# Attention with the probabilities stationary and all query tiles first, and a recurrent layer whose gate tiles run among its convolution tiles

## The reference

```python
# first block, attention: q and k are normed and rotated first
sc = jnp.einsum("bqgrd,bkgd->bgrqk", qi, k).astype(jnp.float32) * scale
p = jax.nn.softmax(sc, axis=-1).astype(v.dtype)
return jnp.einsum("bgrqk,bkgd->bqgrd", p, v)

# second block, recurrent layer
h = rms_norm_2(x, norm_g)
u = h @ w_in
xb, gate = u[..., :D_RNN], u[..., D_RNN:]
xb = causal_depthwise_conv(xb, conv_w, conv_b)
r = jax.nn.sigmoid(... xblk, w_rg ... + b_rg)
i = jax.nn.sigmoid(... xblk, w_ig ... + b_ig)
log_a = -LRU_C * r.astype(jnp.float32) * jax.nn.softplus(-lam.astype(jnp.float32))
a = jnp.exp(log_a)
bterm = jnp.sqrt(-jnp.expm1(2.0 * log_a)) * (i * xb).astype(jnp.float32)
_, hs = lax.associative_scan(_lin_combine, (a, bterm), axis=1)
y = hs.astype(x.dtype) * jax.nn.silu(gate)
return y @ w_out
```

## Time and profile before

| | |
|---|---|
| median of 3 runs | 1882.53 us (1878.83 to 1888.39) |
| the profiled execution: its own time | 1876.38 us |
| the profiled execution: span of its instructions | 1873.7 us, mean granted clock 0.943 |
| PE / DVE / ACT / POOL busy, share of the span | 91% / 59% / 39% / 39% |
| chain that ended last | PE 70%, DVE 16%, issue 4%, ACT 4%, POOL 3%, DMA 2% |

### The profile page before, as it was taken

The page is one execution under the profiler, slowest core; times in us unless marked ns, Lnnn a source line. Parts: engine busy times, 40 slices in busy tenths (PEclk is TensorE's granted clock), DMA queues, the critical chain, the costliest instruction groups (busy, mean ns, idle before and its releaser), DMA issues.

```text
span 1873.7 us, 21281 instructions
## 1 busy us (share of the span) xinstructions
PE 1710.0 (91%) x7890; PEld 1325.2 (71%) x7890; DVE 1113.2 (59%) x1337; ACT 729.1 (39%) x1125; POOL 722.1 (39%) x341
## 2 busy tenths in 40 slices
PE   3889999998979999999989999999898797699997
PEld 2677888887755554688858888888576585577765
DVE  4889999997276877686542121121568825457652
ACT  2256666665324433322233232233465333322322
POOL 1134454444641221254634444445233362323324
PEclk8889999999978888999999999999999899889999
DMA  7133333333210000356513232232222132201102
GB/s 300 39 121 110 123 114 121 116 113 101 79 45 23 22 13 11 122 206 218 184 56 102 90 102 91 100 100 92 68 71 76 56 101 73 68 24 56 56 28 75
DMA packets 43404, 171.71 MB, mean 92 GB/s; under 512 B 4592, under 2 KB 4976, under 8 KB 39984
## 3 DMA queue, kind: packets, MB, share of 16 engines
q1 hardware_dynamic: 36144, 133.86, 21.1%
q10 hardware_dynamic: 7168, 36.57, 5.7%
HBM read 168.19 MB, written 2.23 MB: 91 GB/s over the span
## 4 chain that ended last, share of the span: by engine, by line
PE 70%; DVE 16%; issue 4%; ACT 4%; POOL 3%; DMA 2%; SPq 0%; DVEq 0%; ACTq 0%; POOLq 0%
PE bank L944 20%; PE bank L945 19%; PE bank L946 19%; PE bank L1141 3%; POOL w_lo L506 2%; PE bank L1116 2%; DMA ada_piece<-ada 1%; DVE rstd L1383 1%; DVE tmp L1453 1%; DVE xb_conv L1792 1%; PE bank L1294 1%; DVE xb_conv L1747 1%; PE bank L1076 1%; DVE tmp L1401 1%; PE bank L983 1%
## 5 line engine op out<-in xcount | busy, mean ns | idle before, releaser
L506 POOL TENSOR_TENSOR w_lo<-w_raw,w_hi 128x1024 fp32r<-128x1024 f32 x230 | 605.9, 2639 | 916.4 <-ACT w_hi L547 916.2
L944 PE MATMUL bank<-a_hi,w_hi 128*128 128x512 f32 x1040 | 424.8, 408 | 40.6 <-POOL w_lo L506 17.5
L945 PE MATMUL bank<-a_lo,w_hi 128*128 128x512 f32 x1040 | 415.8, 400 | 0.0
L946 PE MATMUL bank<-a_hi,w_lo 128*128 128x512 f32 x1040 | 414.5, 399 | 0.0
L547 ACT ACTIVATE w_hi<-w_raw 128x1024 fp32r<-128x1024 f32 x230 | 239.8, 1049 | 147.4 <-PE bank L946 144.7
L944 PEld LDWEIGHTS bank<-a_hi,w_hi 128*128 128x128 f32 x1040 | 201.9, 194 | 98.6 <-issue 23.2
L944 PE MATMUL bank<-b_hi,w_hi 128*128 128x512 f32 x600 | 237.8, 396 | 2.2 <-DVE b_lo L1804 1.4
L945 PE MATMUL bank<-b_lo,w_hi 128*128 128x512 f32 x600 | 234.6, 391 | 0.0
L946 PE MATMUL bank<-b_hi,w_lo 128*128 128x512 f32 x600 | 234.6, 391 | 0.0
L946 PEld LDWEIGHTS bank<-a_hi,w_lo 128*128 128x128 f32 x1040 | 201.6, 194 | 44.0
L945 PEld LDWEIGHTS bank<-a_lo,w_hi 128*128 128x128 f32 x1040 | 202.3, 194 | 41.0 <-issue 0.7
(11 more groups left out here) (311 smaller groups left out, 2611.5 us busy)
## 6 DMA issues: line engine op xcount, KB each, us to landing
w_raw<-ws SPq DMA_DIRECT2D x230, 512.0 KB, 3.3
cs_rows<-cs_scratch ACTq DMA_DIRECT2D x16, 1024.0 KB, 5.2
ada_piece<-ada ACTq DMA_DIRECT2D x16, 1024.0 KB, 5.4
ada_piece<-ada SPq DMA_DIRECT2D x8, 1024.0 KB, 14.9
x_stream<-x SPq DMA_DIRECT2D x1, 2048.0 KB, 16.6
x_stream<-x ACTq DMA_DIRECT2D x1, 2048.0 KB, 8.5
out<-x_stream SPq DMA_DIRECT2D x8, 256.0 KB, 2.1
rope_table<-rope ACTq DMA_DIRECT2D x1, 512.0 KB, 4.4
```

Of the source, the lines that this page charges most:

```text
L506: nc.gpsimd.tensor_tensor(wlo[b][:, :], raw[b][:, :], r32(whi[b][:, :]), ALU.subtract).then_inc(lo_done, 1)
L944: mm(out, lh, rh, start=first, stop=False)
L945: mm(out, lh, rl, start=False, stop=False)
L946: return mm(out, ll, rh, start=False, stop=last)
```

## The change

**Attention.** All ten k and q tiles are computed before the first head, none in the loop; the rotated q tiles are kept whole in `q_full`. The three score products of 65 rows become two: `k_hi_over_lo` (the high part over the low part, 128 rows) by `q_hi_twice`, and `k_hi` with a row of ones (65 rows) by `q_lo`, which carries the maximum. The product for the maximum has the 128 rows too. For the values the probabilities are stationary: for each chunk of keys four matmuls, each with a 128 x 128 block of probabilities loaded and 65 columns of values and ones moving. The output is tokens by features, with each token's sum in a column; DVE inverts 128 x 4 sums and scales 4 x 64 columns, and after two heads PE turns the result back with four transposes (`turn_pair`). `row_of_max` transposes a broadcast of 128 columns. POOL no longer adds the rotation's two products; DVE does.

**Recurrent layer.** The tiles of the stream are split with the gain alone while the MLP's last tiles come in (`gain_low`), so the `xb` tiles need not wait for the root; each `xb` and `gt` tile is scaled by the inverse root in PSUM by DVE (`scale_tile`) when it is done. The order of tiles is `RNN_STEPS`: after `gates` 4 the first five roots are taken, and `gt` 0 to 4 run among `xb` 7 to 9 and the last gates; five more `gt` follow at the end. The convolution's low part is made one step later.

The diff, cut to its core:

```diff
@@ -27,12 +27,13 @@
...
-Q_RING = 6
+Q_RING = 4
...
+    steps = []
+    for n in range(RT + RNN_LAG):
+        if n >= RNN_HALF + RNN_LAG:
+            steps.append(("gt", n - RNN_HALF - RNN_LAG))
+        if n < RT:
+            steps.append(("xb", n))
+        if n >= RNN_LAG:
+            steps.append(("gates", n - RNN_LAG))
+    return steps + [("gt", n) for n in range(RT - RNN_HALF, RT)]
...
+            kHL = [sb(f"k_hi_over_lo{g}", [P, SEQ], F32R) for g in range(N_KV)]
             kH = [sb(f"k_hi{g}", [HD + 1, SEQ], F32R) for g in range(N_KV)]
-            kL = [sb(f"k_lo{g}", [HD + 1, SEQ], F32R) for g in range(N_KV)]
...
-                pool.wait_ge(rot_step, 2 * (j + 1))
-                nc.gpsimd.tensor_tensor(t[3][:, :], t[3][:, :], t[2][:, :], ALU.add).then_inc(rope_done, 1)
...
+                mm(M[i % 2][:, :], qHH[h % Q_RING][:, i * P:(i + 1) * P], kHL[h // 4][:, :], start=True,
...
+                    ins = nc.tensor.transpose(ROW[:, i * P:(i + 1) * P], mx[h % 2][:, i:i + 1].broadcast_to([P, P]), ident)
...
-                split_mm(S[n % 2][:, :], kH[g][:, w], kL[g][:, w], qH[b][:, :], qL[b][:, :], True,
-                         True).then_inc(qk_done, 1)
+                mm(S[n % 2][:, :], kHL[g][:, w], qHH[b][:, :], start=True, stop=False)
+                mm(S[n % 2][:, :], kH[g][:, w], qL[b][:, :], start=False, stop=True).then_inc(qk_done, 1)
...
             def values(h, c):
                 pe.wait_ge(exp_done, NCH * h + c + 1)
-                if c == 0 and h:
-                    pe.wait_ge(o_ev, h)
-                mm(OP[:, :], vv[:, c, h // 4, :], PT[:, c, :], start=(c == 0), stop=(c == NCH - 1)).then_inc(pv_done, 1)
...
+                if c == 0 and h >= 2:
+                    pe.wait_ge(o_ev, h - 1)
+                W = HD + 1
+                for i in range(NCH):
+                    ins = mm(OQ[h % 2][:, i * W:(i + 1) * W], PT[:, c, i * P:(i + 1) * P], vv[:, c, h // 4, :],
+                             start=(c == 0 and i == 0), stop=(c == NCH - 1 and i == NCH - 1))
+                ins.then_inc(pv_done, 1)
...
+            def turn_pair(u):
...
+                for i in range(NCH):
+                    ins = nc.tensor.transpose(OT[:, i * P:(i + 1) * P], t[4 + u % 2][:, i * P:(i + 1) * P], ident)
+                ins.then_inc(turned, 1)
...
+            for n, name in enumerate(QK):
+                feature_tile(name, in_a, in_a_lo)
+                if n:
+                    stat(QK[n - 1], 0, blk64)
+                if n == KVT:
+                    value_tiles()
+                if name == ("q", QT - 3):
+                    pe.wait_ge(y_ev, PAIRS)
+                    for i in range(2):
+                        scores_for_max(0, i)
+                if name == ("q", QT - 2):
+                    for i in range(2, NCH):
+                        scores_for_max(0, i)
+            for name in [("v", c) for c in range(NCH)] + QK[-2:]:
+                wait_evac(pe, name)
             row_of_max(0)
-            stat(QK[KVT + 1], 0, blk64)
-            for c in range(NCH):
-                wait_evac(pe, ("v", c))
+            stat(QK[-1], 0, blk64)
             for h in range(N_Q):
-                u = h // 2
                 for c in range(NCH):
                     scores(h, c)
                     if h + 1 < N_Q:
                         scores_for_max(h + 1, c)
-                if h % 2 == 0 and u + 2 < QT:
-                    feature_tile(("q", u + 2), in_a, in_a_lo)
+                if h % 2 == 0 and h:
+                    if h == 2:
+                        pe.wait_ge(std_ready, NORM_AT[QK[-1]] + 1)
+                    turn_pair(h // 2 - 1)
...
-                    if c == 0 and h + 1 < N_Q:
+                    if c == 1 and h + 1 < N_Q:
                         row_of_max(h + 1)
-                    if c == 1 and h % 2 == 0 and u + 2 < QT:
-                        stat(("q", u + 2), 0, blk64)
...
+            for kind, n in RNN_STEPS:
+                if kind == "gates":
+                    for w in ("rg", "ig"):
+                        feature_tile((w, n), lambda k: xH[n % XB][:, :], lambda k: xL[n % XB][:, :], (rdyX, n))
+                else:
+                    feature_tile((kind, n), in_a, in_a_lo, (rdyA, 2 * KT))
+                if (kind, n) == ("xb", 0):
+                    stat("na", KT - 1)
...
+            def share(h):
+
...
+                out = t[4 + u % 2][:, :].rearrange("p (b f) -> p b f", b=NCH)[:, :, h % 2 * HD:(h % 2 + 1) * HD]
+                inv = inv_den[h % 2]
...
-                V.tensor_tensor(t[4 + u % 2][:, :], t[4 + u % 2][:, :], sums[:, :], ALU.mult).then_inc(pair_ready, 1)
-                ve.wait_ge(pair_ready, u + 1)
+                V.tensor_tensor(out, o[:, :, 0:HD], inv[:, :, None].broadcast_to([P, NCH, HD]), ALU.mult).then_inc(o_ev, 1)
 
...
+                ve.wait_ge(rot_step, 2 * (QK_AT[name] + 1))
+                v(V.tensor_tensor(t[3][:, :], t[3][:, :], t[2][:, :], ALU.add))
+                v.settle()
...
+                if h == 1:
+                    turn_q(QT - 2)
+                    swap_halves(QK[-1])
+                    inverse(QK[-1], src=std_last)
+                if h == 3:
+                    turn_q(QT - 1)
+                if h + Q_RING - 1 < N_Q:
+                    split_q(h + Q_RING - 1)
+                if h % 2 == 0 and h:
+                    split_pair(h // 2 - 1)
+                share(h)
...
+                    if f == FQ - 1 and m:
+                        gain_low("na", m - 1, aL, aH, hiA, 2 * KT, rdyA)
...
+            def halve(first):
+                variance(first)
+                variance(first + 1)
+                for n in range(first, first + RNN_HALF):
+                    scale_x(n)
+                    if n + 2 < first + RNN_HALF:
+                        variance(n + 2)
+
+            for kind, n in RNN_STEPS:
+                if kind == "xb":
+                    scale_tile(("xb", n), rstd, xb_scaled)
+                    if n:
+                        conv_low(n - 1)
+                    conv_taps2(n)
+                elif kind == "gates":
+                    gate_x(n)
+                    decay(n)
+                    if n + 1 == RT - RNN_LAG:
+                        conv_low(RT - 1)
+                    if n % RNN_HALF == RNN_HALF - 1:
+                        halve(n + 1 - RNN_HALF)
+                else:
+                    scale_tile(("gt", n), rstd, gt_scaled)
+                    recurrence(n)
+                    gate_y(n)
+                    y_low(n)
```

377 lines of the change are left out of this document (191 added, 186 removed).

## The result

The kernel before took 1883.19 us (median of 4 runs), the changed one 1796.11 (1785.55 to 1802.97). The ratio is 0.9532, with a 95% interval from 0.9469 to 0.9594. The forecast was 1948, slower; the case that came was the first rival, full clock, for which the text had 1835 and a chance of 0.11. Between the two profiled executions (1876.38 and 1802.97, the slowest of its four) lie 73 us: 49 in the attention and 23 in the recurrent layer. The other 14 of the 87 between the medians are the other executions'; what differs among those is taken up with e8.

A forecast was written before the change was run, and what follows sets the result against it. PE carries 70% of the chain: attention hangs on matmul cost and clock, the recurrent layer on DVE and order. 1876.4 + 74 (attention at half clock) - 9 (recurrent layer) = 1941, plus 6.1 to the median: 1948; range 1885 to 1985, own range 1915 to 1980.

The forecast's parts named there:

- the first rival, full clock: Head loop: 128-row score products keep the clock up, `ga` 0 at 728, time 1835 us; chance 0.11.
- Ahead of the loop: Before the head loop: ten tiles must be finished, DVE is later than PE, loop starts at 585, bounds 574 and 592.
- The stall at head 2: Head loop: PE waits 2 to 3 us at head 2 for maxima that DVE takes late behind its q tile work.
- The clock: Head loop: half clock for all 16 heads, 15.8 us each, attention +74 us; chance 0.69.
- The rule of the Trainium skill: Head loop: idle gaps between matmuls lower the clock, so a nearly gapless loop would keep full clock.
- Scores: Head loop: three products a chunk instead of four, 1.08 us at full clock, 1.87 at half; 15 us saved at full.
- Values: Head loop: 32 records a head with 128 x 128 loads, 3.6 us at full clock and 7.0 at half.
- the case in which it costs the same at both: Head loop: a value record costs at half clock what it does at full, 1894 us; within mixed case's chance 0.11.
- A head: Head loop: scores, values and transposes sum to 8.6 us at full clock, 15.8 at half.
- The earlier start: Recurrent layer: `xb` 0 runs without waiting for the root, so the first `scale_tile` stands 8.6 us earlier.
- The roots: Recurrent layer: roots stay 22.5 us and pay one more ACT start of 2.7 for being split: 25.
- the recurrences: Recurrent layer, end: recurrences stay 54.4 us and get ten scalings of the `gt` tiles: 61.4.

The follow-up runs named there:

- e8: Changed kernel with VectorE's work on the last two q tiles moved from head 1 (and 3) to heads 3, 5 and 7: 1790.99 us, ratio 0.9558.
- e3: Changed kernel with the product for the maximum on 64 rows in place of 128: 1915.12 us, ratio 1.0201.
- e5: Changed kernel with the product for the maximum on 65 rows in place of 128: 1831.39 us, ratio 0.9758.
- e6: Changed kernel with all score products on 65 rows, three for scores and one for the maximum, new values kept: 1905.13 us, ratio 1.015.
- e4: Changed kernel with TensorE's old score and value forms, maximum on 64 rows, no q tiles in the loop: 1853.18 us, ratio 0.9872.
- e11: e4 with the product for the maximum on 65 rows in place of 64: 1806.60 us, ratio 0.9629.
- e9: e8 plus six idle 128-row products ahead of the first scores and six after head 0's second chunk: 1784.94 us, ratio 0.9514.

## Why the prediction was wrong, step by step

**Ahead of the loop** was right: 585 forecast, 586.0 measured. DVE sets it up to 573; the last 12 us are PE's last q tile, which had waited for DVE's maxima, and the chain behind it, where the forecast had DVE to the end.

**The stall at head 2** was right in its place and its releaser, 2 to 3 us forecast, 4.59 measured. Of the difference 1.55 is the one cast beside POOL.

**The clock** is the step that failed. "Nothing of the kind that raised it comes until `ga` 0" was wrong: the new scores are of that kind. I had read from rows 7 that gapless work of 65 rows lets the clock fall and that 128-row products lift it, and had then counted only the dense q tiles as such, though I wrote that two thirds of the scores now have 128 rows. e3, e5 and e6 give what was missing. With the new values and every score product on 65 rows the loop is at 0.50 to its end; with one product in three on 128 rows it is so for half of the heads; with two in three, as the change makes it, for about a head and a half at a time. That it took dense q tiles was wrong even for the kernel before. In these stretches of its loop the clock fell and came back while PE did head 1's values and head 2's scores, the next q tile beginning only at 587.75:

```profile
576.00:579.00 3.00, 3.00 (x7) 1.19 (x7) 2.38 (x5) 0.60 (x1) 0.86 (x1) 0.60 0.00 0
...
582.00:585.00 3.00, 3.00 (x10) 1.48 (x9) 2.21 (x4) 1.16 (x2) 0.00 (x0) 1.00 0.00 0
```

and e4, without q tiles, does the same to its end. The loop that was forecast is that of a kernel that differs by one operand: its 1948 belongs beside e3's 1915. The weight was wrong: 0.69 against 0.11 for a question on which the trace of before had no row (no stretch of scores with 128 rows), and which it could only bound from both sides.

**The rule of the Trainium skill** on idle gaps ("TensorE: Matmul & The Clock Gate", section "HAM oscillation — how this bites in real kernels") named the side that came. As a reason it holds in part. In the changed kernel each fall did follow a wait (1.33 us at the entry, 4.59 at head 2). But before, the clock fell at 614 without one, in e8 waits of 1.34 and 1.57 us were followed by no fall, and in e6 the clock stayed down for 224 us without a gap, so the absence of gaps did not lift it.

**Scores.** 1.08 us a chunk at full clock was 0.73, and 1.87 at half was 1.28. The step "four products took 1.31, one of them 0.23, three are left: 1.08" took away a product and kept 0.38 us that belonged to the 64-row product beside those of 65, which the change removes. 4 x 0.23 is 0.92: that the four did not add up to 1.31 was to be seen in rows 4. Over 64 chunks it is 64 x 0.35 = 22 us at full clock, and 64 x 0.59 = 38 at half: even the case that was forecast would have come out that much lower.

**Values** were right at full clock: 3.6 forecast from rows 6, 3.44 measured; at half clock 7.0 and, by 16 records in 3.3 us, 6.6. A record cost 0.206 us there and 0.108 at full, so the case in which it costs the same at both did not come. **A head** was thus 7.0 for 8.6. With that the rival's own sum, 728 for `ga` 0, would have been 586 + 16 x 7.0 + 5 = 703. The other 15 us up to 718 are the first four heads, which took 633.6 - 586.0 = 47.6 us for 28, the stall among it, less some 4 of the 5 us allowed behind the last head. Two bounds were also slightly off: by the terms given, the forecast's own range runs from 1918 to 1988, not from 1915 to 1980.

**Recurrent layer.** The earlier start was right: 8.6 us forecast, 9.2 measured (1337.10 less the attention's 49.0, against 1278.88). From there 157.4 was forecast and 143.9 measured. The roots were mis-sized: 25 for what took 6.6 and 6.5 in two groups. The 22.5 of before held multiplications of 2.9 us that ran into POOL's `w_lo` (L1740, mean 1340 ns for 687 now). That is 12 of the 13.5 us. In the recurrences the sum copied a mean too: each scan was to go on taking 2.25 us, and it takes 1.22. But that is not all gain, as collisions came up at other instructions: 6.1 us at the addition of one (L1863) and 6.0 at the convolution's low part (L1848).

## What to carry to other kernels

Before you subtract one instruction from a group, see whether the group adds up to its instructions; what is over belongs to something, here to a 64-row matmul beside those of 65, and goes or stays with that. Where a clock has two levels, a change that makes TensorE's work thinner or denser can be worth more than its instructions: one product on 64 rows cost 119 us against 128 rows, and 84 against 65, in a loop whose values move 65 columns at a time. And where an engine's instruction is far longer than its like, ask what runs beside it: a schedule moves such collisions, and a sum that copies the old means keeps them.

## What the runs showed of the hardware that I had not expected

- A float32 score product of 64 rows next to one of 65 or 128 costs 0.1 to 0.2 us on either side, 0.38 us a chunk at full clock (1.31 in the kernel before, 0.90 in e11) and 0.6 at half (1.88 in e3, 1.28 in e5). 65 beside 128 rows costs nothing. Whether it is the change of rows or the 64 rows themselves is open: no run has products of 64 rows alone.
- The granted clock went with the rows that the products use. With PE busy throughout, loops of the same kinds of instructions stayed at 0.50 for 224 us (all scores at 65 rows, e6), for 107 us (one product in three at 128, e5) and for 13 to 16 us (two in three at 128, the changed kernel), all with the new form of the values; with the old form, 512 columns moving, 65 rows were enough for full clock from 620 on (e11). It can come back without any denser work ahead of it, as at 692 in e5. What exactly is looked at stays open.
- A wait of 1.58 us was followed by 0.50 in e9's profiled execution and one of 1.57 at the same place in e8's was not; so for 1.33 and 1.34 at the entry. Executions of one kernel lie 12 to 17 us apart, and their mean granted clock goes with it (0.965 and 0.955). That it is such waits in each of them is likely but not shown, since only one execution of each has a trace.
